# One step of a chunked RWKV-7 scan: state increments for two heads in one 128-row product, zero-padded keys and bonus rows, and input transfers spread over the steps

## The reference

```python
def step(S, inp):
    r_t, w_t, k_t, v_t, a_t, b_t = inp
    Sa = jnp.einsum('bhvk,bhk->bhv', S, a_t)
    S = S * w_t[:, :, None, :] + Sa[..., None] * b_t[:, :, None, :] + v_t[..., None] * k_t[:, :, None, :]
    y = jnp.einsum('bhvk,bhk->bhv', S, r_t)
    return S, y
```

## Time and profile before

| what | value |
|---|---|
| median of three executions | 1442.89 us (1441.17 to 1444.55) |
| profiled execution, its own time | 1442.76 us |
| its span | 1441.0 us |
| PE busy | 1376.4 us, 96% |
| DVE, ACT, POOL busy | 723.8, 618.8, 538.6 us |
| L935 (`value_h`) | 224 records, 14.8 us busy |
| L1000 (`answer_h`) | 224 records, 11.8 us busy |

### The profile page before, as it was taken

One profiled execution on the slowest core, in us unless ns is written; L12 is line 12 of the kernel. 1 busy time (PEld: TensorE's weight loads), 2 busy tenths in 40 slices (PEclk: granted clock), 3 DMA queues, 4 the chain that ended last, 5 costly groups with the idle time before them and its releaser, 6 DMA issues.

```text
span 1441.0 us, 23198 instructions
## 1 busy us (share of the span) xinstructions
PE 1376.4 (96%) x9043; PEld 1151.4 (80%) x9043; DVE 723.8 (50%) x1118; ACT 618.8 (43%) x924; POOL 538.6 (37%) x307
## 2 busy tenths in 40 slices
PE   6999998889999999999999999999999999999998
PEld 4777787775888888888888787766888888888887
DVE  6899988567463301433168453287563301342163
ACT  7886536454433211333264432486432312332252
POOL 3110012215444453444442343346434443445342
PEclk9999999999999999999999999999999999999999
DMA  6222100301332333223232422200222333233321
GB/s 201 73 73 88 59 1 4 126 4 59 95 105 93 117 102 117 88 87 117 87 125 89 147 88 88 88 1 31 88 88 88 117 116 103 88 104 101 105 99 59
DMA packets 119902, 126.45 MB, mean 88 GB/s; under 512 B 6268, under 2 KB 114556, under 8 KB 119816
## 3 DMA queue, kind: packets, MB, share of 16 engines
q1 hardware_dynamic: 119120, 123.99, 26.4%
q10 hardware_dynamic: 376, 0.61, 0.2%
q0 software_dynamic: 320, 0.66, 0.2%
HBM read 123.12 MB, written 2.12 MB: 87 GB/s over the span
## 4 chain that ended last, share of the span: by engine, by line
PE 69%; DVE 9%; issue 5%; ACT 5%; POOL 1%; ACTq 0%; POOLq 0%; DVEq 0%
PE pb L633 19%; PE pb L635 19%; PE pb L634 19%; DVE xl L2479 3%; ACT whi L1484 2%; PE pb L1357 1%; PE pb L1325 1%; POOL wlo L528 1%; PE pb L1327 1%; PE pb L1326 1%; PE pb L763 1%; PE pb L1384 1%; PE pb L1366 1%; DVE X L2471 1%; ACT xh L1495 1%
## 5 line engine op out<-in xcount | busy, mean ns | idle before, releaser
L525 POOL TENSOR_TENSOR wlo<-wraw,whi 128x1024 fp32r<-128x1024 f32 x94 | 224.7, 2390 | 619.9 <-ACT whi L1484 488.5
L633 PE MATMUL pb<-xh,whi 128*128 128x512 f32 x1088 | 419.2, 385 | 6.4 <-DVE xl L2129 2.7
L634 PE MATMUL pb<-xl,whi 128*128 128x512 f32 x1088 | 412.4, 379 | 0.0
L635 PE MATMUL pb<-xh,wlo 128*128 128x512 f32 x1088 | 412.4, 379 | 0.0
L1484 ACT ACTIVATE whi<-wraw 128x2048 fp32r<-128x2048 f32 x108 | 206.3, 1910 | 255.6 <-PE pb L635 252.5
L633 PEld LDWEIGHTS pb<-xh,whi 128*128 128x128 f32 x1088 | 205.5, 189 | 58.7 <-issue 16.2
L528 POOL TENSOR_TENSOR wlo<-wraw,whi 128x1024 fp32r<-128x1024 f32 x94 | 230.7, 2454 | 0.0
L635 PEld LDWEIGHTS pb<-xh,wlo 128*128 128x128 f32 x1088 | 205.6, 189 | 29.1
L634 PEld LDWEIGHTS pb<-xl,whi 128*128 128x128 f32 x1088 | 205.6, 189 | 28.4 <-issue 1.0
L633 PE MATMUL pb<-hid_h,whi 128*128 128x512 f32 x512 | 194.3, 380 | 0.0
L634 PE MATMUL pb<-hid_l,whi 128*128 128x512 f32 x512 | 194.0, 379 | 0.0
(11 more groups left out here) (324 smaller groups left out, 1790.0 us busy)
## 6 DMA issues: line engine op xcount, KB each, us to landing
wraw<-in_mlp_w_dram SPq DMA_DIRECT2D x128, 512.0 KB, 4.3
wraw<-in_rwkv_w_rkvo_dram SPq DMA_DIRECT2D x32, 512.0 KB, 4.3
wraw<-in_ple_w_gate_dram SPq DMA_DIRECT2D x16, 512.0 KB, 4.4
xtok<-in_x_dram SPq DMA_DIRECT2D x8, 512.0 KB, 6.3
wraw<-in_diff_w_q_dram SPq DMA_DIRECT2D x8, 512.0 KB, 3.9
wraw<-in_w_k_shared_dram SPq DMA_DIRECT2D x8, 512.0 KB, 4.3
wraw<-in_w_v_shared_dram SPq DMA_DIRECT2D x8, 512.0 KB, 4.2
wraw<-in_diff_w_o_dram SPq DMA_DIRECT2D x8, 512.0 KB, 3.9
```

Source lines behind the costliest of these rows:

```text
L525: pool.tensor_tensor(wlo[:, par, front], wraw[:, par, front], whi[:, par, front].bitcast(F32), ALU.subtract)
L633: mm(o, wh, ah, start=first, stop=False)
L634: mm(o, wh, al, start=False, stop=False)
L635: return mm(o, wl, ah, start=False, stop=last)
```

## The change

The increment of a tile is one product over all 128 partitions for both heads, in place of two of 64 by 64. For this the stationary operand is 128 by 128 with its off-diagonal quarters zero. `value_h` gets it from two column blocks of the key tile (`K2`, blocks 3 and 4 of `KV`, which grows from 4 to 5 blocks and puts the values in block 2). `answer_h` gets it from new tiles `Bd`, written by `b_taken` in place of columns of `NL`. POOL clears these tiles once before the scan with six memsets; ACT waits for that three times (`k_zero`). `kv_turn` swaps the places of keys and values in its bank. On SP's queue, the second to fourth transfer of x, the two of `rwkv_g2` and the first of the output weights each wait for the next `y_mm` of chain 1. Tile addresses move; unused semaphores go.

```diff
-        W3 = 3 * CH
-        KV = [at(f"KV{k}", o, [P, QUAD, 4 * CH]) for k, o in enumerate((W_HI, W_LO + 8192, W_HI + 5120, W_LO + 13312))]
+        K2 = slice(3 * CH, 5 * CH)
+        KV = [at(f"KV{k}", o, [P, QUAD, 5 * CH]) for k, o in enumerate((W_HI, W_LO + 8192, W_HI + 5120, W_LO + 13312))]
...
+        Bd = [at(f"Bd{k}", REST + 1024 + 2048 * k, [P, QUAD, 2 * CH]) for k in range(2)]
...
-            n0 = QUAD * (q % HALF)
-            return NL[q // HALF][ROWS[h], n0:n0 + QUAD, 0:CH]
+            return Bd[q % 2][ROWS[h], :, ROWS[h]]
...
             for t in range(TT):
+                if t:
+                    sp.wait_ge(s.y_mm[1], HALF + t)
                 sp.dma_start(xtok2[:, t, :], x[0, t * P:(t + 1) * P, :]).then_inc(s.x2_in, 16)
...
-            load(N_G2, 0, [(r0[:, 0:1024], rwkv_g2[0][0:128, :]), (r0[:, 1024:2048], rwkv_g2[0][32:160, :])])
+            sp.wait_ge(s.y_mm[1], HALF + 4)
+            load(N_G2, 0, [(r0[:, 0:1024], rwkv_g2[0][0:128, :])])
+            sp.wait_ge(s.y_mm[1], HALF + 5)
+            load(N_G2, 0, [(r0[:, 1024:2048], rwkv_g2[0][32:160, :])])
+            sp.wait_ge(s.y_mm[1], HALF + 6)
             square(rwkv_w_rkvo[0, 3], N_WO)
...
             pool.wait_ge(s.pe_step, 8 * N_G2)
+            for k in range(4):
+                pool.memset(KV[k][:, :, K2], 0.0).then_inc(s.k_zero, 1)
+            for k in range(2):
+                pool.memset(Bd[k][:, :, :], 0.0).then_inc(s.k_zero, 1)
...
                 if k % HALF < HALF - 1:
-                    kv = KV[k % 4]
-                    for h in range(2):
-                        u, r = 2 * x + i, SWAP[h]
-                        ins = mm(h_part(x, i, ROWS[h]), kv[r, u, CH:2 * CH], kv[r, u, W3:W3 + CH], start=False, stop=False,
-                                 skip_group_check=True)
+                    kv, u = KV[k % 4], 2 * x + i
+                    ins = mm(h_part(x, i, slice(0, P)), kv[:, u, K2], kv[:, u, 2 * CH:3 * CH], start=False, stop=False,
+                             skip_group_check=True)
...
-                    n = QUAD * (k % HALF) + 2 * x + i
-                    for h in range(2):
-                        r = ROWS[h]
-                        ins = mm(h_part(x, i, r), NL[k // HALF][r, n, 0:CH], Us[x][r, i, :], start=False, stop=True,
-                                 skip_group_check=True)
+                    ins = mm(h_part(x, i, slice(0, P)), Bd[k % 2][:, 2 * x + i, :], Us[x][:, i, :], start=False, stop=True,
+                             skip_group_check=True)
...
+                if b in (0, 2):
+                    act.wait_ge(s.k_zero, b + 2)
...
-                        ins = A(kv[SWAP[h], :, 1:4:2, :], turned[ROWS[e], :, :, h, :], ACT.Copy)
+                        ins = A(kv[SWAP[h], :, 2:4 + h:1 + h, :], turned[ROWS[e], :, :, h, :], ACT.Copy)
...
+                    if q == 0:
+                        act.wait_ge(s.k_zero, 6)
```

More of the change, by code:

```diff
@@ L211, in trunk @@
         KB_BEFORE = (0, 0, 0, 1, 3, 3, 4, 4)
-        W3 = 3 * CH
-        W3 = 3 * CH
-        KV = [at(f"KV{k}", o, [P, QUAD, 4 * CH]) for k, o in enumerate((W_HI, W_LO + 8192, W_HI + 5120, W_LO + 13312))]
-        TiT = [at(f"TiT{k}", o, [P, QUAD, CH]) for k, o in enumerate((W_HI + 4096, W_LO + 12288))]
+        K2 = slice(3 * CH, 5 * CH)
+        KV = [at(f"KV{k}", o, [P, QUAD, 5 * CH]) for k, o in enumerate((W_HI, W_LO + 8192, W_HI + 5120, W_LO + 13312))]
+        TiT = [at(f"TiT{k}", W_HI + 14336 + 1024 * k, [P, QUAD, CH]) for k in range(2)]
         NB = HALF * QUAD
@@ L226, in trunk @@
         Xc = at("Xc", REST, [P, QUAD, CH])
-        assert REST + 4096 <= XX
+        Bd = [at(f"Bd{k}", REST + 1024 + 2048 * k, [P, QUAD, 2 * CH]) for k in range(2)]
+        assert REST + 5120 <= XX
         Hs = [at(f"Hs{k}", W_HI + 10240 + 2048 * k, [P, 2, 2, CH]) for k in range(2)]
@@ L270, in trunk @@
         names = """gnc_in raw0 raw1 w_hi w_lo pe_step cst_in cst2_in x_in0 x_in1 x_in2 x_in3 rows_in hrows_in x2_in p_in lam_in hot_in
-            rel_in bvec_out strip_in out_st x_tr x_sq x_rt x_rs x_dg dx par_tr par_ev small_set edge_set w_sub gains lam_s lam_e
-            h_ready h_act wa_in x_edge mix_b x_hi x_ready dx_v acc norm_ps norm_rt dense_a dense_v act_link vec_link pool_link
+            rel_in bvec_out strip_in out_st x_tr x_sq x_rt x_rs x_dg dx par_tr par_ev small_set edge_set w_sub lam_s lam_e
+            h_act wa_in x_edge mix_b x_hi x_ready dx_v acc norm_ps norm_rt dense_a dense_v vec_link pool_link
             w_mix lora_hi lora_rdy g_cum dec exps kk_sq kk_ps kk_rt kk_rs kb_ps kn pa prep
-            bs_mm nl_raw nl_mask inv_ld inv_lk inv_d tdg
+            bs_mm nl_raw nl_mask inv_ld inv_lk inv_d tdg k_zero
             x_unit kv_mm kv_ev bt_mm bt_ev lo_ev vz0 vz1 vb0 vb1 ks_mm ll_ev x5_mm xb_ev t5_mm tt_ev
@@ L821, in kv_turn @@
                 for i in range(2):
-                    pe.transpose(pb[F1][:, 2 * i * P:(2 * i + 1) * P], St[:, K_, c + i, t], ident)
+                    pe.transpose(pb[F1][:, (2 * i + 1) * P:(2 * i + 2) * P], St[:, K_, c + i, t], ident)
                 if b == 0:
@@ L825, in kv_turn @@
                 for i in range(2):
-                    ins = mm(pb[F1][:, (2 * i + 1) * P:(2 * i + 2) * P], St[:, V_, c + i, t], centre[:, :], start=True, stop=True)
+                    ins = mm(pb[F1][:, 2 * i * P:(2 * i + 1) * P], St[:, V_, c + i, t], centre[:, :], start=True, stop=True)
                 ins.then_inc(s.kv_mm, 1)
@@ L911, in value_z @@
                     u, r = 2 * x + i, SWAP[h]
-                    ins = mm(z_part(x, i, ROWS[h]), kv[r, u, 0:CH], kv[r, u, W3:W3 + CH], start=i == 0, stop=False,
+                    ins = mm(z_part(x, i, ROWS[h]), kv[r, u, 0:CH], kv[r, u, 2 * CH:3 * CH], start=i == 0, stop=False,
                              skip_group_check=True)
@@ L923, in value_y @@
                     u, r = 2 * x + i, SWAP[h]
-                    ins = mm(y_part(x, i, ROWS[h]), kv[r, u, W3:W3 + CH], kv[r, u, 2 * CH:W3], start=i == 0, stop=False,
+                    ins = mm(y_part(x, i, ROWS[h]), kv[r, u, 2 * CH:3 * CH], kv[r, u, CH:2 * CH], start=i == 0, stop=False,
                              skip_group_check=True)
@@ L2333, in local_scores @@
                     dve.wait_ge(s.vb[1], q - 3)
-                tt(KV[q % 4][:, :, :].rearrange("p u (b t) -> p u b t", t=CH)[:, :, 0:3:2, :],
-                   pb[F2][:, :].rearrange("p (u b t) -> p u b t", b=2, t=CH), tri.rearrange("p u (b t) -> p u b t", t=CH), ALU.mult)\
+                tt(KV[q % 4][:, :, 0:2 * CH], pb[F2][:, :].rearrange("p (u t) -> p u t", t=2 * CH), tri, ALU.mult)\
                     .then_inc(s.ll_ev, 1)
```

## The result

The changed kernel takes 1466.57 us (median of four executions, 1464.41 to 1470.09), the kernel before beside it 1442.03 (1440.02 to 1444.55): a ratio of 1.0173, 95% interval 1.0150 to 1.0196. It is slower by 24 us. The forecast was 1466.

What follows compares the result with a forecast made beforehand. PE was taken to bound the second half's plain steps, PE and DVE together steps 1 to 5. Products +27, transfers -4 and memsets 0 gave +23 us on 1442.76: forecast 1466, range 1447 to 1478.

Steps and rivals of the forecast that it cites:

- A pair of 64-row products is cheap: At A, B and C, removing eight 64-row pairs saves PE only 0.12 us a step, since most run beside partners.
- 16 records of 0.11: Eight 128-row products add 1.76 us of PE a step; last records of five groups may leave 0.05 earlier, -0.27.
- Passage of 0.29: Going from 64-row to 128-row work and back costs PE 0.29 us; five excursions a step, 1.45.
- Rival (a): Width costs but passage doesn't: 1.64 us a step, plain step 7.1, kernel 1451; chance 0.14.
- The take_y wait fills up: A 128-row value_h with its passage fills PE's wait for take_y of chain 0, taking 0.36 us off a step.
- A step of 8.2: A plain step goes from 5.8 to 8.2 us: less 0.36 of wait, plus 2.8 of PE work.
- +17 and +9 for the halves: Scan: second half grows by 7 x 2.4 = 17 us, steps 1 to 5 by 5 x (8.2 - 6.4) = 9.
- Transfers, -4: Spreading SP's transfers one to a step ends PE's late instructions and lower clock in steps 8 and 9, saving 4 us.
- +27 for the products: In the scan, the 128-row products add 17 us, 9 us, and 1 us for steps 0 and 6 together.
- (b): Records cost alike, so 16 fewer save 0.43 us a PE-bound step; with the transfers, 1435; chance 0.10.
- (c): Width at its lower bound and no passage: 0.84 us a step, no change, 1442; chance 0.04.
- (d): The transfers' cure fails, each meeting an instruction fetch, and widths are at their upper bound: 1470 to 1479; chance 0.07.

Runs made afterwards that it cites:

- e4_no_value_h: The kernel before without the value_h products, so its output lacks the v k term of the state: 1440.09 us.
- e6_grouped_64_rows: The kernel before, 64-row products and transfers in one burst, with products of a kind grouped together at places A and B: 1442.26 us.
- e5_answer_h_only: The changed kernel with value_h put back to two 64-row products and answer_h alone over 128 rows: 1449.03 us.
- e3_grouped: The changed kernel with its eight 128-row products of a step in three groups instead of five: 1452.51 us.
- e9_take_y_after: The changed kernel with take_y of chain 0 put ahead of take_u of chain 1 on ACT: 1456.92 us.
- e2_products_only: The changed kernel with SP's queue as it was before, so the 128-row products alone: 1467.27 us.
- e1_spread_only: The kernel before with only the new waits on SP's queue, which spread the transfers one a step: 1438.31 us.
- e7_split_answer_h: The changed kernel with answer_h of chain 1 split by a k_score pair at place C, one excursion more: 1465.21 us.
- e12_take_z_earlier: e11_grouped_spread_take_y with take_z of chain 0 between the second and third of ACT's four copies of keys and values: 1437.94 us.
- e11_grouped_spread_take_y: The kernel before with spread transfers, grouped order at A and B, and take_y of chain 0 ahead of take_u of chain 1: 1438.07 us.

## Why the prediction was right, step by step

- **A pair of 64-row products is cheap: right.** Without four of the eight pairs a step is 0.2 us shorter (e4_no_value_h). The term for lost sharing at A (-0.12) can't be told apart; e6_grouped_64_rows shows that sharing doesn't hang on the order that I read it from.
- **16 records of 0.11: right** (0.23 a product in e5_answer_h_only). The allowance of -0.27 for last records was wrong: the last L942 in front of L921 starts at some 314.14 (0.11 after the one at 314.03), and L921 0.21 later, as late as L990 stood behind the last L826, a record of 128 moving columns.
- **Passage of 0.29: right**, from one against two products in an excursion and, as 0.33 with what neighbours lose, from e3_grouped. Rival (a) is out.
- **The take_y wait fills up: wrong.** I wrote that a wide `value_h` fills the wait, and did not see that ACT reaches `take_y` only behind `take_u` of chain 1, which waits for the solve behind place A. Place A grew, the solve moved with it, and the wait went from 0.36 to 0.44 beyond a tier. e9_take_y_after showed both its cause and its price.
- **A step of 8.2: it is 8.0, in part by luck.** The forecast's terms, by place, were 1.23 for A, 0.91 for B, 0.68 for C and -0.36 for the wait. A measured +1.29 and B +0.96, so these are right. C measured +0.04: I hadn't counted that PE waits there already, for ACT's copies and `take_z`, and the wide products filled that wait (read from the timelines; no run took the wait from the wide kernel). The stretch from A to B, with the `take_y` wait in it, went from 1.04 to 1.08, not down by 0.36. Two terms wrong by -0.64 and +0.40 nearly cancel. The rest, -0.14 on average, is mostly late instructions inside `state_z` of chain 1, which I hadn't counted either: L952 waits for issue twice in steps 10 to 13 of before, 0.5 in all by the waits and 0.8 by the starts, and the changed kernel has no such wait.
- **+17 and +9 for the halves.** Steps 1 to 5: +9.8, one of them at a clock of 0.83. Steps 0 and 6: +0.9 where 1 was forecast. Steps 8 to 14, transfers included: +12.6 where 17 - 4 was forecast; steps 10 to 13 of them +8.75 where 9.6 was forecast. DVE did cease to bound the first half.
- **Transfers, -4: right alone (-4.4), wrong in company.** With wide products they give 0.7, within scatter. The statement that step 9 would have its full clock was wrong: 0.75. The stall did go, but e2_products_only has none even with the burst, and 7.2 us at half clock took the place of what there was to gain.
- **+27 for the products: they cost 24.6** by the medians. The lower clock is in it on both sides: 14.4 us at 0.53 in e2_products_only (steps 0, 1, 8 and 9), 7.6 us at 0.53 to 0.57 in the kernel before (steps 6 and 9). That the total came out within 1 us of the forecast is luck as to its parts: the products cost some 2 less than forecast and the transfers gave 3 less.
- **Memsets at 0: right.** In POOL's timeline the six take 2.85 us in all, near the lower bound. The first `take_z` starts at 219.2 instead of 218.9, but so it does in e1_spread_only, which has no memsets:

```profile
205.48 1.92 POOL L561 MEMSET KV<- 128x512 f32 x4 [117.19 <-PE pb L644]
207.34 0.99 POOL L563 MEMSET Bd<- 128x512 f32 x2
```

- **Rivals.** (a) is out by the passages. (b) is out: 16 fewer records a step, and 2.2 us more time. (c) is out with both of its halves. (d) is out by its time, but half of it came true: widths were near their upper bound, and the transfers' cure gave nothing beside them, though by the clock and not by new waits for issue. The Trainium skill ("TensorEngine Tiling (Array Packing)", Key Properties) has a change of the tiling mode drain the engine. The rows agree that the change costs time, 0.29 us per excursion in e5_answer_h_only as in the changed kernel; that this time is a drain no row shows.

## What to carry to other kernels

Ask of the old products what they cost where they stand, from the distance between starts: two 64 by 64 products in different quarters of the array were nearly free here, and one product over all 128 rows in their place cost 0.23 us plus 0.29 for each passage in and out, so group such products or leave them out. Before a longer stretch is said to fill a wait, follow the waiting engine's own queue back: here ACT's order carried the wait along, and turning two lines of it took 0.49 us off a step. Where the clock or late instructions move about between kernels, compare plain steps at full clock; a total can hide 5 us.

## What the runs showed of the hardware

- **The lower clock came with PE busy.** The changed kernel has 0.53 (the lower level, 1.2 GHz, in nearly all of it) from 227.6 to 231.2 and from 289.2 to 296.4. PE is busy in all of both stretches, and the last idle time in front of each is a wait for `take_y` of 0.52 us that ends at 225.08 and 288.22. e3_grouped and e7_split_answer_h have the same wait at the same places (0.5 to 0.65 us) and kept their full clock all through the scan. Elsewhere it came behind longer idle time: in step 6 of the kernel before behind 2.04 us, in steps 6 and 7 of e9_take_y_after behind 1.44 us (0.51 from 269.6 to 280.0). I found no rule; what sets it stays open.
- **Partners pair across a few products of the program**, so a pair doesn't need its partner next to it (e6_grouped_64_rows).
- **Something sets a floor for the 64-row kernels, and it stays open what.** In e6_grouped_64_rows and e12_take_z_earlier what shortened a plain step came back as waits for issue, of up to 2.9 us with the burst and 1.2 us with DMA busy at only 0.3; smaller transfers didn't help. In e11_grouped_spread_take_y it came back without such waits. That four kernels end at 1438 would fit late instructions, but no run makes the instructions arrive earlier, and steps that differ by 0.1 us don't show in medians whose executions scatter by 3 to 5 us.
